# State-space sums in four row strips, head means as turned rows, and the tables of turns made earlier

## The chip, the cores and the metric

One core of a Trainium2 chip runs the whole program. The metric is the device time of one execution in microseconds (us); the figure for a kernel is the median of its runs. The engines are TensorE (PE), whose loads of the stationary operand are a row of their own (PEld), VectorE (DVE), ScalarE (ACT), GpSimd (POOL) and SyncE (SP), which issues most transfers.

## The reference, cut to what matters

Two hybrid layers (attention, convolution, retention, MLP), and then a second block: differential attention on queries and keys that are normed for each head and rotated, beside a state-space branch, then a gated MLP. The change lies in the projection part of the second block:

```python
q = rope(rmsnorm(q, q_norm_gain[i]), cos, sin)
k = rope(rmsnorm(k, k_norm_gain[i]), cos, sin)
...
bu_re = jnp.einsum('blgc,gpc->blgp', uf, bb_re)
bu_im = jnp.einsum('blgc,gpc->blgp', uf, bb_im)
_, _, xr, xi = lax.associative_scan(_complex_affine_combine, (ar, ai, bu_re, bu_im), axis=1)
y = (jnp.einsum('gcp,blgp->blgc', c_re, xr) - jnp.einsum('gcp,blgp->blgc', c_im, xi) + d_skip * uf)
```

The complex recurrence is done on every fourth position. Its input is turned back by an angle that grows with time (`sin_n`, `cos_n`), so that what is left to scan is real, and the result is turned forward again.

## The kernel before, in words

Weights come as f32 in units of 128x2048. ACT makes a rounded high part of each unit (`hi`, `w_hi`), POOL the rest (`lo`, L518, `w_lo`), and PE makes each product from three terms (L711, 128x512 each). All orders are written out by hand. In the q and k part, PE works through 32 accumulations of 12 matmuls each (four groups of `feature_major(4)`), and after accumulation p it calls `hook(p)`, which puts the small matmuls of the side work in between. ACT and DVE walk through the same p in programs of their own. A semaphore for each PSUM bank says that it is full (`full4`) or free (`free4`); each engine waits in program order.

The side work by p, on PE: `sums_in(blk)` at 8, 12, 16, 20 (L1010, input of the recurrence for a block of four strips of 32 rows); `sums_out(blk)` at 14, 18, 22, 26 (L1024 and L1031, output, bank 6); `short_response` at 10 (L995, bank 6); `q_columns(n)` at 9 and 17 (L1041, bank 7, means of q's squares as columns); `k_mean(j)` from 22 on (L1051, bank 7). On DVE: `states(blk, stage)` with stages 0, 1, 2 at the three p after each `sums_in` (L2341 to L2349 read the banks, L2355 is the scan, L2360 to L2366 make the state that `sums_out` needs); `skip(q)` (L2371, frees bank 6) one p after `sums_out`; `rotate(j)` (L2398, L2400, L2401) at 8, 8, 12, 12, 16, 16, 20, 20 for q, then for k with `k_norm`. At one p the order on DVE is skip, states, rotate, q_columns. On ACT at one p: `block_out`, `short_response` (four copies, L1723), then `jobs(p)`, which begins with `fetch_partner(j)`: four transfers (L1692) that need the rotation of block j-2 (`q_ready`), two such sets at p = 10 and at p = 18.

`sums_in` uses banks 4 and 5, a bank for each of the parts (real, imaginary). Two strips run at a time, and after each round PE waits (`strip_done`) so that two strips never write one bank together. POOL makes the tables `sin_n` and `cos_n` with `turns(b)`, six TENSOR_TENSOR each (L643 to L648), between the `lo` calls of this part, two buffers of each table, so that turns(2) and turns(3) wait for the states of blocks 0 and 1.

Of the kernel before, what the change touches and what calls it, by code (L numbers as in the profile page):

```python
# [186 lines left out]
def build(nc, a, out):  # L187

    with ExitStack() as ctx:
        m = memory(nc)  # L190
        m.bank = [ctx.enter_context(nc.psum_tensor(f"bank{i}", [P, T], F32)) for i in range(8)]
# [38 lines left out]
    "taps_clear", "u_ready", "strip_done", "spread", "kernel_made", "glu_done",  # L230
# [46 lines left out]
def memory(nc):  # L277
# [43 lines left out]
    def ar(name, shape, kb, dt=F32):  # L321
# [37 lines left out]
    m.b_part = ar("b_part", [P, T], 24)  # L359
# [6 lines left out]
    m.both = put("both", [P, T], at=x_at + 2048 * 5)  # L366
    m.sin_n, m.cos_n = ([put(f"{name}{i}", [P, T], at=x_at + 2048 * (6 + k) if i == 0 else arena + 1024 * (36 + 2 * k)) for i in range(2)]
                        for k, name in enumerate(("sin_n", "cos_n")))
# [3 lines left out]
    m.q_mean, m.q_power = (ar(name, [P, 2, 8, NT], 72 + 2 * i) for i, name in enumerate(("q_mean", "q_power")))  # L372
    m.g_hi, m.g_lo = (ar(f"gated{i}", [P, 4, T], 76 + 8 * i, F32R) for i in range(2))
# [123 lines left out]
def low_parts(pool, m, s):  # L497
# [89 lines left out]

    def layer(l):
# [17 lines left out]
        if l < DEPTH - 1:  # L606
            passes(pool, c, U_MLP // 2 - 2, PER_PAIR, pair)
        else:
            for _ in range(4):
                lo()  # L610
            for _ in output_tables():
                lo()
            for _ in range(U_MLP - 4 - 4 - 15):
                lo()
# [14 lines left out]
    def turns(b):  # L629

        shape = [P, 4, TURN_A, TURN_B]
        wide = lambda x: x[:].rearrange("p (s a b) -> p s a b", s=4, a=TURN_A)
        sin, cos, both = wide(m.sin_n[b % 2]), wide(m.cos_n[b % 2]), wide(m.both)
        of = slice(4 * b, 4 * b + 4)
        (sa, sb), (ca, cb) = ((x[:, of, 0:TURN_A].rearrange("p s (a o) -> p s a o", o=1).to_broadcast(shape),
                               x[:, of, TURN_A:].rearrange("p s (o b) -> p s o b", o=1).to_broadcast(shape)) for x in (m.sin_t, m.cos_t))
        if b == 0:

            pool.wait_ge(s["x_parked"], 16)
        if b >= 2:  # L640

            pool.wait_ge(s["state_ready"], 2 * (b - 1))
        pool.tensor_tensor(sin, sa, cb, ALU.mult)  # L643
        link(pool.tensor_tensor(both, ca, sb, ALU.mult))
        link(pool.tensor_tensor(sin, sin, both, ALU.add))
        pool.tensor_tensor(cos, ca, cb, ALU.mult)
        link(pool.tensor_tensor(both, sa, sb, ALU.mult))
        link(pool.tensor_tensor(cos, cos, both, ALU.subtract))  # L648
        pool.sem_inc(s["turned"], 1)


# [30 lines left out]
def products(pe, m, s):  # L682
# [316 lines left out]
    def sums_in(blk):  # L999

        fill(4)
        fill(5)
# [3 lines left out]
        for r in range(4):  # L1006
            for j in range(SUB):
                for part in range(2):
                    q = (r + part) % 4
                    mm = pe.matmul(bank[4 + part][:, q * P:(q + 1) * P], m.b_pow[strips[q], SUB - 1 - j, part, blk, :],  # L1010
                                   m.uT[strips[q], blk, j * N_SUB:(j + 1) * N_SUB], start=(j == 0), stop=(j == SUB - 1))
                    if j == SUB - 1:
                        mm.then_inc(s["strip_done" if r < 3 else f"full{4 + part}"], 1)
            if r < 3:
                pe.wait_ge(s["strip_done"], c.up("strip_done", 2))
# [19 lines left out]
    def q_columns(n):  # L1035
# [18 lines left out]
    def hook(p):  # L1054
# [4 lines left out]
        for blk in range(4):  # L1059
            if p == SUMS_IN_AT[blk]:  # L1060
                sums_in(blk)
            if p == SUMS_OUT_AT[blk]:
                sums_out(blk)
        for n in jobs_at(p, COLUMNS_AT):
# [205 lines left out]
COLUMNS_AT, COLUMN_ROOT_AT = (9, 17), 18  # L1270
# [39 lines left out]
def functions(act, a, m, s):  # L1310
# [362 lines left out]
    def block_out(b, j):  # L1673
# [4 lines left out]
        elif j >= 4:  # L1678
            act.wait_ge(s["q_columns"], j // 4)
        act.activation(m.q_square[j % 4][:], bank[b][:], ACT.Square).then_inc(s["q_squared"], 1)  # L1680
# [21 lines left out]
    def jobs(p):  # L1702

        for j in jobs_at(p, PARTNER_AT):
            fetch_partner(j)
        for n in jobs_at(p, COLUMNS_AT):
# [22 lines left out]
    for p in range(32):  # L1729
# [11 lines left out]
        if p in SUMS_IN_AT:  # L1741
            use(4, 5)
# [157 lines left out]
def arithmetic(dve, m, s):  # L1900
# [432 lines left out]
    def states(blk, stage):  # L2333

        w0, w1, w2 = (x[:] for x in m.w)
        sin, cos = m.sin_n[blk % 2][:], m.cos_n[blk % 2][:]
        if stage == 0:
            dve.wait_ge(s["turned"], blk + 1)
            full(4)
            full(5)  # L2340
# [3 lines left out]
            link(dve.tensor_tensor(w1, bank[5][:], sin, ALU.mult))  # L2344
            link(dve.tensor_tensor(w0, w0, w1, ALU.add))
            dve.tensor_tensor(w1, bank[5][:], cos, ALU.mult).then_inc(s["free5"], 1)
            freed(4)
            freed(5)
# [62 lines left out]
    def jobs(p):  # L2411

        for j in jobs_at(p, ROTATE_AT):
            rotate(j)
        for n in jobs_at(p, COLUMNS_AT):
# [272 lines left out]
```

## Time and profile before

| what | value |
| --- | --- |
| median of 3 runs | 2146.66 us (2142.12 to 2146.75) |
| the profiled execution, its own time | 2144.72 us |
| its span in the trace | 2142.9 us |
| PE busy | 98% of the span |
| DVE, ACT, POOL busy | 50%, 41%, 43% |
| mean granted TensorE clock | 0.99 |

Busy shares are over the whole span. What the change touches lies at 1270 to 1430 us of the trace, and there the shares are others. A row of a timeline has the start in us, the duration in us, the engine, the line, the operation with its operands, and the count; in brackets stands how long the engine was idle before it, and what it waited for.

### The profile page before, as it was taken

The page shows a single profiled execution, that of the slowest core. Times are in us where ns is not written, and L with a number is a line of the kernel's source. Part 1 is how long each engine was busy: PE and PEld are TensorE (multiplying, and loading weights), DVE is VectorE, ACT ScalarE, POOL GpSimd, SP SyncE. Part 2 cuts the span into 40 slices and gives each one's busy share as a digit, 9 for nine tenths or more (in the row PEclk, how much of TensorE's full clock was granted, in tenths as well). Part 3 has the DMA queues.
Part 4 walks back from the last instruction along what each step waited for, and adds up shares of the span by engine and source line. Part 5 has one row for each costly group of instructions (what it writes and reads, how often), then busy time and mean ns, then how long its engine had stood idle before and what let it go on. Part 6 is the DMA issues. An engine that isn't in the chain of part 4 may idle for free.

```text
span 2142.9 us, 27507 instructions
## 1 busy us (share of the span) xinstructions
PE 2100.7 (98%) x10200; PEld 1676.2 (78%) x10200; DVE 1061.5 (50%) x1725; ACT 876.3 (41%) x1219; POOL 925.4 (43%) x306
## 2 busy tenths in 40 slices
PE   8999999999999999999999999999999899999999
PEld 7875888888888776888888888877766787888887
DVE  5866242222247654422222258985588534554555
ACT  5345462223243445533222343164566534333332
POOL 5522444443455333545654456333312254444442
PEclk9999999999999999999999998899999999999999
DMA  5431213223224331233222242223111232322232
GB/s 182 150 117 71 77 63 98 97 98 98 99 69 149 125 93 46 79 99 98 94 100 87 92 148 85 66 84 108 60 60 60 95 100 81 97 88 90 97 98 78
DMA packets 120050, 202.29 MB, mean 94 GB/s; under 512 B 6544, under 2 KB 51856, under 8 KB 119696
## 3 DMA queue, kind: packets, MB, share of 16 engines
q1 hardware_dynamic: 112992, 189.12, 26.7%
q10 hardware_dynamic: 6960, 11.88, 1.9%
q8 instruction: 60, 0.98, 0.2%
q14 instruction: 38, 0.31, 0.0%
HBM read 189.44 MB, written 8.12 MB: 92 GB/s over the span
## 4 chain that ended last, share of the span: by engine, by line
PE 75%; issue 16%; POOL 3%; DVE 3%; ACT 1%; ACTq 1%; DMA 0%; POOLq 0%; DVEq 0%; SPq 0%
PE bank L711 63%; PE bank L813 5%; POOL w_lo L518 3%; PE bank L822 1%; PE bank L1010 1%; PE bank L765 1%; PE bank L840 1%; PE bank L880 1%; PE bank L774 1%; PE bank L868 0%; ACTq L1572 0%; DVE pr L2018 0%; PE bank L1041 0%; ACTq L1692 0%; PE bank L906 0%
## 5 line engine op out<-in xcount | busy, mean ns | idle before, releaser
L518 POOL TENSOR_TENSOR w_lo<-raw,w_hi 128x2048 fp32r<-128x2048 f32 (+1 forms) x167 | 741.9, 4442 | 1119.3 <-ACT w_hi L1356 1119.3
L711 PE MATMUL bank<-act_hi,w_hi 128*128 128x512 f32 x1488 | 595.6, 400 | 5.9 <-DVE hid L2561 2.5
L711 PE MATMUL bank<-act_hi,w_lo 128*128 128x512 f32 x1488 | 584.7, 393 | 0.0
L711 PE MATMUL bank<-act_lo,w_hi 128*128 128x512 f32 x1488 | 584.1, 393 | 0.0
L1356 ACT ACTIVATE w_hi<-raw 128x2048 fp32r<-128x2048 f32 (+1 forms) x170 | 314.2, 1848 | 591.2 <-PE bank L711 545.8
L711 PEld LDWEIGHTS bank<-act_hi,w_hi 128*128 128x128 f32 x1488 | 282.5, 190 | 78.0 <-issue 11.8
L711 PEld LDWEIGHTS bank<-act_hi,w_lo 128*128 128x128 f32 x1488 | 281.9, 189 | 60.7
L711 PEld LDWEIGHTS bank<-act_lo,w_hi 128*128 128x128 f32 x1488 | 282.5, 190 | 58.2 <-issue 1.4
L711 PE MATMUL bank<-h_hi,w_hi 128*128 128x512 f32 x704 | 277.7, 394 | 0.3 <-DVE x L2526 0.3
L711 PE MATMUL bank<-h_lo,w_hi 128*128 128x512 f32 x704 | 277.4, 394 | 0.0
L711 PE MATMUL bank<-h_hi,w_lo 128*128 128x512 f32 x704 | 277.4, 394 | 0.0
L2263 DVE TENSOR_TENSOR f<-f,bank 128x512 f32<-128x512 f32 x128 | 88.1, 688 | 238.7 <-PE bank L711 238.7
L2249 DVE SCALAR_TENSOR_TENSOR hid<-bank,rrow 128x512 f32<-128x512 f32 x64 | 43.7, 691 | 250.3 <-PE bank L711 245.3
L711 PEld LDWEIGHTS bank<-h_hi,w_hi 128*128 128x128 f32 x704 | 131.7, 187 | 33.4 <-DVE h_lo L2080 0.7
L711 PEld LDWEIGHTS bank<-h_hi,w_lo 128*128 128x128 f32 x704 | 131.7, 187 | 32.7
L711 PEld LDWEIGHTS bank<-h_lo,w_hi 128*128 128x128 f32 x704 | 131.7, 187 | 32.1
L2556 DVE TENSOR_TENSOR bank<-bank,rrow 128x512 f32<-128x512 f32 x44 | 30.7, 699 | 142.9 <-PE bank L711 140.4
L813 PE MATMUL bank<-act_hi,w_hi 128*128 128x512 f32 x192 | 76.3, 398 | 5.7 <-DVE act_lo L1940 5.2
L534 POOL TENSOR_TENSOR sums<-sums,squares 128x512 f32<-128x512 f32 x50 | 64.6, 1292 | 37.4 <-ACT squares L1374 35.1
L1993 DVE SCALAR_TENSOR_TENSOR bank<-ypad,lcol,bank 128x512 f32<-128x512 f32 x116 | 76.6, 755 | 0.0
L813 PE MATMUL bank<-act_hi,w_lo 128*128 128x512 f32 x192 | 74.8, 390 | 0.0
L813 PE MATMUL bank<-act_lo,w_hi 128*128 128x512 f32 x192 | 74.8, 389 | 0.0
(362 smaller groups left out, 2638.5 us busy)
## 6 DMA issues: line engine op xcount, KB each, us to landing
raw<-in_w_up SPq DMA_DIRECT2D x32, 1024.0 KB, 5.4
raw<-in_w_down SPq DMA_DIRECT2D x32, 1024.0 KB, 5.0
raw<-in_w_in SPq DMA_DIRECT2D x26, 1024.0 KB, 5.1
raw<-in_w_up SPq DMA_DIRECT2D x44, 512.0 KB, 4.6
raw<-in_w_in SPq DMA_DIRECT2D x28, 768.0 KB, 4.5
raw<-in_w_out SPq DMA_DIRECT2D x12, 1024.0 KB, 5.0
raw<-in_w_down SPq DMA_DIRECT2D x22, 512.0 KB, 4.2
raw<-in_w_attn_proj SPq DMA_DIRECT2D x4, 1024.0 KB, 5.1
```

What stands on the lines that cost most here:

```text
L518: pool.tensor_tensor(m.w_lo[slot][:, 0:n], m.raw[slot][:, 0:n], m.w_hi[slot][:, 0:n].bitcast(F32), ALU.subtract).then_inc(s["split_ready"], 1)
L534: ins = pool.tensor_tensor(m.sums[:], m.sums[:], m.squares[n % 4][:], ALU.add)
L711: mm = pe.matmul(o, ll if i == 2 else lh, rl if i == 1 else rh, start=first and n == 0, stop=last and n == len(steps) - 1)
L765: mm = pe.matmul(bank[b][:, t:t + 1], x[:, t * P:(t + 1) * P], m.per_d, start=(part == 0), stop=(part == 1))
L774: mm = pe.matmul(bank[b][:, t * P:(t + 1) * P], column[:, t:t + 1].to_broadcast([P, P]), m.ident, start=True, stop=True)
L813: mm = pe.matmul(bank[b][:], (wl if i == 2 else wh)[:, k % KU, cols], (m.act_lo if i == 1 else m.act_hi)[:, k, :], start=(k == 0 and i == ...
L822: pe.matmul(bank[b][:] if o is None else o, lhsT, rhs, start=True, stop=True).then_inc(s[f"full{b}"], 1)
L1356: act.activation(m.w_hi[slot][:, 0:n], m.raw[slot][:, 0:n], ACT.Copy).then_inc(s["w_hi"], 1)
L1993: ins = dve.scalar_tensor_tensor(to, y, w, sums, ALU.mult, ALU.add)
L2249: dve.scalar_tensor_tensor(m.hid[:, b, :], bank[b][:], 0.0, m.rrow[:], ALU.max, ALU.mult).then_inc(s[f"free{b}"], 1)
L2263: dve.tensor_tensor(sums, sums, bank[4 + b][:], ALU.add).then_inc(s[f"free{4 + b}"], 1)
L2556: dve.tensor_tensor(bank[b][:], bank[b][:], m.rrow[:], ALU.mult).then_inc(s["up_scaled"], 1)
```

## The change

`sums_in` now gives each of the four row strips a bank of its own (banks 4 to 7, one tensor of four banks), real part in columns 0 to 127, imaginary part in 128 to 255. The rounds and their waits go. All four banks must be free before it, and DVE frees all four after its last read of stage 0.

q's means: `q_rows` (p = 10 and 18) makes one matmul of 512 columns for each of the four squares, into a column strip of bank 7; ACT copies the bank into `q_rows`; `q_columns` (p = 11 and 19) turns it with four matmuls. There were 32 matmuls for each n before. The root of the columns moves from p = 18 to p = 20.

The tables have four buffers. turns(0) is made in the MLP of the second layer, in three pieces between `lo` calls; turns(1) stands behind the second layer's norm ahead of the `lo` that turns(0) followed before; turns(2) and turns(3) stand where turns(0) and turns(1) stood. Only turns(3) waits for `x_parked`. ACT's `block_out(7)` waits for all four.

```diff
+        m.quad = ctx.enter_context(nc.psum_tensor("bank4", [P, 4, T], F32))
+        m.bank += [m.quad[:, i, :] for i in range(4)]
...
-    m.b_part = ar("b_part", [P, T], 24)
+    m.b_part = ar("b_part", [P, T], 10)
...
+            lo()
+            for _ in turns(0):
+                lo()
+            for _ in range(U_MLP - 4 - 4 - 15 - 3):
                 lo()
...
     lo()
     pool.wait_ge(s["arena_free"], DEPTH + 1)
     pool.memset(m.taps[:], 0.0).then_inc(s["taps_clear"], 1)
-    pool.wait_ge(s["trig_ready"], 2)
+    whole(turns(1))
     lo()
-    turns(0)
+    whole(turns(2))
     lo()
-    turns(1)
-    lo()
-    turns(2)
-    lo()
-    turns(3)
-    lo()
-    lo()
+    whole(turns(3))
+    for _ in range(4):
+        lo()
     lo()
...
     def sums_in(blk):
-        fill(4)
-        fill(5)
+        for b in QUAD:
+            fill(b)
...
-        for r in range(4):
+        for part in range(2):
             for j in range(SUB):
-                for part in range(2):
-                    q = (r + part) % 4
-                    mm = pe.matmul(bank[4 + part][:, q * P:(q + 1) * P], m.b_pow[strips[q], SUB - 1 - j, part, blk, :],
+                for q, b in enumerate(QUAD):
+                    mm = pe.matmul(bank[b][:, part * P:(part + 1) * P], m.b_pow[strips[q], SUB - 1 - j, part, blk, :],
                                    m.uT[strips[q], blk, j * N_SUB:(j + 1) * N_SUB], start=(j == 0), stop=(j == SUB - 1))
...
+    def q_rows(n):
         pe.wait_ge(s["q_squared"], c.up("q_squared", 4))
         fill(7)
         for j in range(4):
-            for t in range(NT):
-                mm = pe.matmul(bank[7][:, 0:8 * NT].rearrange("p (c j t) -> p c j t", c=2, t=NT)[:, :, j, t], m.q_square[j][:, t * P:(t + 1) * P],
-                               m.blk64.rearrange("p (c d) -> p c d", c=2)[:, :, 0], start=True, stop=True)
+            mm = pe.matmul(bank[7][strips[j], :], m.blk64.rearrange("p (c d) -> p c d", d=4)[:, :, 0], m.q_square[j][:], start=True, stop=True)
+        mm.then_inc(s["full7"], 1)
+
+    def q_columns(n):
+        fill(7)
+        for t in range(NT):
+            mm = pe.matmul(bank[7][:, 0:8 * NT].rearrange("p (c j t) -> p c j t", c=2, t=NT)[:, :, :, t], m.q_rows[:, t * P:(t + 1) * P],
+                           m.ident.rearrange("p (j c d) -> p j c d", j=4, c=2)[:, :, :, 0], start=True, stop=True)
         mm.then_inc(s["full7"], 1)
...
-COLUMNS_AT, COLUMN_ROOT_AT = (9, 17), 18
+QUAD = (4, 5, 6, 7)
+ROWS_AT, COLUMNS_AT, COLUMN_ROOT_AT = (10, 18), (11, 19), 20
...
         for j in jobs_at(p, PARTNER_AT):
             fetch_partner(j)
+        for n in jobs_at(p, ROWS_AT):
+            evac(7, m.q_rows[:])
...
-            dve.tensor_tensor(w0, bank[4][:], cos, ALU.mult).then_inc(s["dve_step"], 1)
-            dve.tensor_tensor(w2, bank[4][:], sin, ALU.mult).then_inc(s["free4"], 1)
+            dve.tensor_tensor(by_strip(w0), re, by_strip(cos), ALU.mult).then_inc(s["dve_step"], 1)
+            dve.tensor_tensor(by_strip(w2), re, by_strip(sin), ALU.mult)
...
+            link(dve.tensor_tensor(by_strip(w1), im, by_strip(cos), ALU.mult))
+            for b in QUAD:
+                dve.sem_inc(s[f"free{b}"], 1)
```

## Rows read from the trace of the kernel before

**Rows 1.** The page: busy time of each engine, share of the span

```profile
PE 2100.7 (98%) x10200; PEld 1676.2 (78%) x10200; DVE 1061.5 (50%) x1725; ACT 876.3 (41%) x1219; POOL 925.4 (43%) x306
```

**Rows 2.** Windows: length, busy time of each engine, granted clock, DMA share

```profile
1290.00:1380.00 90.00, 88.89 (x732) 74.16 (x731) 79.43 (x92) 19.04 (x25) 54.59 (x29) 0.86 0.26 81
```

**Rows 3.** Timeline of PE, the small matmuls of p = 8 to 14

```profile
1296.73 5.93 PE L1010 MATMUL bank<-uT,b_pow 32*128 32x128 f32 x64
...
1307.48 4.15 PE L1041 MATMUL bank<-cmat,q_square 128*128 128x2 f32 x32
...
1316.89 2.09 PE L995 MATMUL bank<-ctab,braw 128*32 128x128 f32 x64
...
1324.58 4.92 PE L1010 MATMUL bank<-uT,b_pow 32*128 32x128 f32 x64
...
1335.00 2.39 PE L1024 MATMUL bank<-uT,taps 128*128 128x128 f32 x20
1337.32 1.52 PE L1031 MATMUL bank<-state,ctab 128*32 128x128 f32 x48
```

**Rows 4.** Timeline of PE, one of the large matmuls at each clock

```profile
1304.47 0.63 PE L711 MATMUL bank<-act_lo,w_hi 128*128 128x512 f32 x1
...
1320.63 0.39 PE L711 MATMUL bank<-act_lo,w_hi 128*128 128x512 f32 x1
```

**Rows 5.** Timeline of DVE, 1268 to 1405 us

```profile
1268.74 2.47 DVE L2288 TENSOR_TENSOR uT<-bank,rrow 128x512 f32<-128x512 f32 x2
...
1299.65 0.86 DVE L2398 TENSOR_TENSOR partner<-partner,rope 128x512 f32<-128x512 f32 x1 [3.59 <-DMA partner<-q]
...
1313.34 0.69 DVE L2346 TENSOR_TENSOR w<-bank,cos_n 128x512 f32<-128x512 f32 x1
...
1325.61 0.69 DVE L2398 TENSOR_TENSOR partner<-partner,rope 128x512 f32<-128x512 f32 x1 [3.65 <-DMA partner<-q]
...
1329.51 4.99 DVE L2401 TENSOR_TENSOR q<-q,partner 128x512 f32<-128x512 f32 x1
...
1338.86 5.25 DVE L2355 TENSOR_TENSOR_SCAN w<-par,w 128x128 f32<-128x128 f32 x8
...
1353.24 0.69 DVE L2398 TENSOR_TENSOR partner<-partner,rope 128x512 f32<-128x512 f32 x1
...
1361.50 0.69 DVE L2341 TENSOR_TENSOR w<-bank,cos_n 128x512 f32<-128x512 f32 x1
...
1366.00 2.63 DVE L2355 TENSOR_TENSOR_SCAN w<-par,w 128x128 f32<-128x128 f32 x8
...
1377.84 0.69 DVE L2398 TENSOR_TENSOR partner<-partner,rope 128x512 f32<-128x512 f32 x1
...
1379.90 0.69 DVE L2398 TENSOR_TENSOR partner<-partner,rope 128x512 f32<-128x512 f32 x1
...
1404.26 0.69 DVE L2366 TENSOR_TENSOR state<-state,w 128x508 f32<-128x508 f32 x1
```

**Rows 6.** Timeline of POOL, one low part and the first step of turns(3)

```profile
1328.78 5.17 POOL L518 TENSOR_TENSOR w_lo<-raw,w_hi 128x2048 fp32r<-128x2048 f32 x1 [14.33 <-ACT w_hi L1356]
...
1353.28 1.56 POOL L643 TENSOR_TENSOR sin_n<-turn_table,turn_table 128x512 f32<-128x512 f32 x1 [0.62 <-DVE state L2366]
```

**Rows 7.** Timeline of ACT at p = 10

```profile
1319.13 2.44 ACT L1723 ACTIVATE taps<-bank 32x512 f32<-32x512 f32 x4 [18.27 <-PE bank L995]
1321.68 5.01 ACTq L1692 DMA_DIRECT2D partner<-q  x8
```

**Rows 8.** Timeline of PE: a wait at p = 30, and a wait with what follows

```profile
1423.38 1.10 PE L1051 MATMUL bank<-q_square,cmat 128*128 128x512 f32 x2 [1.32 <-DVE q_square L2073]
...
1678.02 0.50 PE L711 MATMUL bank<-act_hi,w_hi 128*128 128x512 f32 x1 [2.30 <-DVE act_lo L2080]
...
1679.05 0.62 PE L711 MATMUL bank<-act_lo,w_hi 128*128 128x512 f32 x1
```

**Rows 9.** Windows: a stretch of the second layer's MLP

```profile
960.00:1000.00 40.00, 40.00 (x176) 32.49 (x175) 10.59 (x16) 12.00 (x12) 24.45 (x10) 1.00 0.25 79
```

More of the change, by code:

```diff
@@ L190, in build @@
         m = memory(nc)
-        m.bank = [ctx.enter_context(nc.psum_tensor(f"bank{i}", [P, T], F32)) for i in range(8)]
+        m.bank = [ctx.enter_context(nc.psum_tensor(f"bank{i}", [P, T], F32)) for i in range(4)]
+        m.quad = ctx.enter_context(nc.psum_tensor("bank4", [P, 4, T], F32))
+        m.bank += [m.quad[:, i, :] for i in range(4)]
         m.x_park = nc.dram_tensor("x_park", (P, NT * D), F32, kind="Internal").ap()
@@ L365, in memory @@
     m.state = [put(f"state{i}", [P, 4, N_SUB], at=x_at + 2048 * (3 + i)) for i in range(2)]
-    m.both = put("both", [P, T], at=x_at + 2048 * 5)
-    m.sin_n, m.cos_n = ([put(f"{name}{i}", [P, T], at=x_at + 2048 * (6 + k) if i == 0 else arena + 1024 * (36 + 2 * k)) for i in range(2)]
-                        for k, name in enumerate(("sin_n", "cos_n")))
+    m.both = ar("both", [P, T], 14)
+    m.sin_n, m.cos_n = ([ar(f"{name}{i}", [P, T], at + 2 * k) for i, at in enumerate((36, 28, 24))] +
+                        [put(f"{name}3", [P, T], at=x_at + 2048 * (5 + k))] for k, name in enumerate(("sin_n", "cos_n")))
     m.q_square = [ar(f"q_square{i}", [P, T], 56 + 2 * i) for i in range(4)]
@@ L372, in memory @@
     m.q_mean, m.q_power = (ar(name, [P, 2, 8, NT], 72 + 2 * i) for i, name in enumerate(("q_mean", "q_power")))
+    m.q_rows = ar("q_rows", [P, T], 92)
     m.g_hi, m.g_lo = (ar(f"gated{i}", [P, 4, T], 76 + 8 * i, F32R) for i in range(2))
@@ L586, in output_tables, with turns, whole @@
         pool.sem_inc(s["ctab_made"], 1)
+    def turns(b):
+        shape = [P, 4, TURN_A, TURN_B]
+        wide = lambda x: x[:].rearrange("p (s a b) -> p s a b", s=4, a=TURN_A)
+        sin, cos, both = wide(m.sin_n[b]), wide(m.cos_n[b]), wide(m.both)
+        of = slice(4 * b, 4 * b + 4)
+        (sa, sb), (ca, cb) = ((x[:, of, 0:TURN_A].rearrange("p s (a o) -> p s a o", o=1).to_broadcast(shape),
+                               x[:, of, TURN_A:].rearrange("p s (o b) -> p s o b", o=1).to_broadcast(shape)) for x in (m.sin_t, m.cos_t))
+        if b == 0:
+            pool.wait_ge(s["trig_ready"], 2)
+        if b == 3:
+            pool.wait_ge(s["x_parked"], 16)
+        pool.tensor_tensor(sin, sa, cb, ALU.mult)
+        link(pool.tensor_tensor(both, ca, sb, ALU.mult))
+        yield
+        link(pool.tensor_tensor(sin, sin, both, ALU.add))
+        pool.tensor_tensor(cos, ca, cb, ALU.mult)
+        yield
+        link(pool.tensor_tensor(both, sa, sb, ALU.mult))
+        link(pool.tensor_tensor(cos, cos, both, ALU.subtract))
+        pool.sem_inc(s["turned"], 1)
+    def whole(steps):
+        for _ in steps:
+            pass
     def layer(l):
@@ L627, in low_parts @@
         layer(l)
[L629 to L649, printed above, removed]
     lo()
@@ L1063, in hook @@
                 sums_out(blk)
+        for n in jobs_at(p, ROWS_AT):
+            q_rows(n)
         for n in jobs_at(p, COLUMNS_AT):
@@ L1705, in jobs @@
             fetch_partner(j)
+        for n in jobs_at(p, ROWS_AT):
+            evac(7, m.q_rows[:])
         for n in jobs_at(p, COLUMNS_AT):
@@ L1741, in functions @@
         if p in SUMS_IN_AT:
-            use(4, 5)
+            use(*QUAD)
         if p in SUMS_OUT_AT:
@@ L2414, in jobs @@
             rotate(j)
+        for n in jobs_at(p, ROWS_AT):
+            use(7)
         for n in jobs_at(p, COLUMNS_AT):
```

26 lines of the change are left out of this document (12 added, 14 removed).

## The prediction

> **What bounds the kernel now.** I read the page first: PE is busy 98% of the span [rows 1], so nearly everything that PE does is on the path, and small matmuls count in full. Then the windows over the part that is changed: in 1290 to 1380 us PE is still busy 88.89 of 90 us, but DVE is busy 79.43 of 90, and the granted clock is 0.86 [rows 2]. Two of the 1.2 and 2.4 GHz levels mixed to 0.86 mean 28% of the stretch, 25 us, at half clock. A large matmul there takes 0.63 us in place of 0.39 [rows 4]. The reader is to see that two engines are near full here, and that a saving on one of them is worth only what the other lets through. Last the timelines of PE, DVE, POOL and ACT, to see who is late at which p. At p = 30 PE waits 1.32 us for DVE [rows 8], and before it the third state (its last step at 1404.26 [rows 5]) is ready just in time for `sums_out(3)`. So by the end of the part DVE already sets the pace.
>
> **What PE saves by itself.** `sums_in` takes 4.92 us at full clock [rows 3], 0.077 us for each of 64 matmuls, waits between rounds included. No row shows four row strips at once. The nearest below is L1031, four column strips: 1.52 us for 48, 0.032 each, so 2.0 us. The bound above is L1024, whole-array matmuls of the same width: 2.39/20 = 0.12 us each, so 7.6 us. I take 2.0, since two strips already beat 0.12 by more than a third. Four blocks save 4 x 2.9 = 11.6 us. `q_columns` is 32 matmuls, 4.15 us [rows 3]; in its place stand four of 512 columns in column strips (by L1024 four times 4 x 0.12 = 1.9 us if they go one after another, 0.5 if side by side) and four turning ones, 0.5 us. I take 1.1 in all, so 2 x 3.0 = 6.0 us. If the half clock went too, PE would have 25/2 = 12.6 us more. Together that is 30 us. The Trainium skill (TensorE: Matmul & The Clock Gate, LDWEIGHTS) speaks against the first term: it says that a load of 32x128 weights takes as long as one of 128x128, since the columns count. By it `sums_in` would take 64 x 128/1.2 GHz = 6.8 us as an estimate, longer than now; the trace has 0.077 us a matmul with two strips, less than such a load of 0.107, so it doesn't bear that out for strips that overlap.
>
> **Why it doesn't arrive.** The banks. `sums_in` now takes banks 6 and 7 as well, and DVE frees all four only at the end of its stage-0 reads. So `short_response` (bank 6) and `q_rows` (bank 7) at p = 10 wait for states(0, 0), which they didn't; `sums_out(0)`, `(1)`, `(2)` wait for stage 0 of blocks 1, 2, 3; `sums_in(1)` waits for DVE's q_columns(0), `sums_in(2)` and `(3)` for skip(0) and skip(1). Behind each waiting matmul stand all large ones.
>
> Start of the part. turns(1) now lies at about 1278 to 1285 us, beside DVE's 18 steps for `b_pow`. Steps of POOL and of DVE that read only SBUF hold each other up: six DVE steps beside turns(3) (begun at 1353.28 [rows 6]) lasted 1353.24 to 1361.50, 8.26 us, where two rotates alone take 2 x 2.06 = 4.12 (1377.84 to 1379.90 is one) [rows 5]. That is 0.7 us a step; three to four steps of `b_pow` are hit, so it ends 2 to 3 us later, and `sums_in(0)` starts at 1299 instead of 1296.73 [rows 3]. It ends at 1301; two accumulations of (1335.00 - 1329.50)/2 = 2.8 us (1329.50 is the end of the second L1010 [rows 3]) bring PE to p = 10 at 1306.6. DVE is no earlier than before, because it waited for a transfer until 1299.65 [rows 5] and then has the same two rotates beside the same `lo` and a turns: its last bank read ends at 1313.34 + 0.69 = 1314.0 [rows 5]. PE waits 7.4 us.
>
> After a wait of 2.30 us large matmuls went at 0.62 [rows 8], half clock. So I take half clock for L995: 4.2 us for 2.09 [rows 3], end 1318.3. On ACT the copy of q_rows stands behind the taps (2.44 us) and behind eight transfers (5.01 us) [rows 7]: 1318.3 + 2.5 + 5.0 + 0.6 (one of the four copies of rows 7) = 1326.4. PE's q_columns is in order at 1327.3, DVE's at 1327.6, and only then come rotates 2 and 3, which began at 1325.61 [rows 5]. That is 2.1 us later. Were the clock full, it would be 1325.3, 0.3 earlier. `sums_in(1)` waits for the same step.
>
> From there DVE is the chain, and I keep its ledger up to 1404.26 [rows 5]. Off: the scans of block 1 ran beside turns(2), 5.25 us against 2.63 [rows 5], so -2.6, with 0.2 on the step before them; the six steps beside turns(3), -4.1. Sum -6.9. The long hits of `lo` stay (4.99 us for a step of 0.69 at 1329.51, beside 1328.78 + 5.17 [rows 5, 6]): `lo` is moved with PE, not removed. On: the later start, +2.1. New waits: `sums_out` can start only when stage 0 is over and takes 4.2 us (1335.00 to 1337.32 + 1.52 [rows 3], and 16 more matmuls at 0.03), while DVE has 0.7 + 2.7 us of block work before skip needs it, so about 1 us each at skip(0) and skip(1), +2.0. At skip(2) DVE has k's rotate and norm in between, no wait. Stage 0 reads four banks in runs of 128 columns: I take 0.69 as now (nothing added); the bound above is L2288, whose reads of PSUM with a stride take 2.47/2 = 1.24 [rows 5], 0.55 more x 16 reads = 8.8 us. Four `sem_inc` a block are under 0.3 us, in the range. Sum: -6.9 + 2.1 + 2.0 = -2.8 us at p = 26, and the same at p = 30, where PE waits for DVE in either kernel.
>
> turns(0) costs nothing in the MLP: with the output tables, the same kind of steps, between the `lo` there, PE is busy 40.00 of 40 us and POOL 24.45 [rows 9]; if the cover were gone, a late `lo` would cost its 2.6 us once or twice. `block_out(7)` waits for turns(3), which ends near 1314, 25 us ahead. No transfer is added. Behind p = 30 both orders are the same, PE is ahead of nothing new, and I carry the 2.8 us to the end.
>
> The sum against the profiled execution is 2144.72 - 2.8 = 2141.9 us. That execution is 1.9 under the median of its kernel, so for the median I say 2146.66 - 2.8 = 2143.9.
>
> **The rivals.**
> - *A, the forecast:* DVE's order sets the time, 2143.9; its own range is 2140 to 2148 (full clock at p = 10 gives 2.4, waits at skip that are twice as long cost 2). Chance 0.50.
> - *B, DVE gives more.* The clock stays full at p = 10 (2.4), the 1 us waits vanish (2.0), and a `lo` falls on bank reads instead of SBUF steps once (4.3 us, 4.99 - 0.69): 2.8 + 8.7 = 11.5, so 2135; half of it gives 2140. For it speaks that two `lo` more or less in phase decide it; against, that the one shown hit in full [rows 5, 6], as did four more like it in the stretch. Chance 0.20.
> - *C, slower: half clock at the output sums.* PE waits some 2 to 5 us before `sums_out(0)`, `(1)` and `(2)`, and a wait of 2.30 was enough [rows 8]. Each at half clock is 4.2 us more, and skip hangs on it. One costs 4.2 (2148.1), two 8.4 (2152.3), three 12.6 (2156.5). It decides from three on. For it: the idle times; against: 5.5 us of large matmuls before each wait. The Trainium skill (TensorE: Matmul & The Clock Gate, Part 1) has the same mechanism, idleness between bursts brings the half rate back. Chance 0.14, of this 0.08 over the 0.3%.
> - *D, the strips don't overlap, or strided bank reads are dear.* 7.6 us a block puts PE behind DVE again: 4 x (7.6 - 4.9) = 10.8, less 6.0 for the means and part of the clock: near 2149; dear reads give 2143.9 + 8.8 = 2152.7. Chance 0.08. The Trainium skill's rule on weight loads (TensorE: Matmul & The Clock Gate, LDWEIGHTS) would be this case.
> - *E, no change:* what is won at p = 30 is lost at a later wait for DVE or ACT. 2146.7. Chance 0.08.
>
> **How the numbers follow.** 0.3% is 6.4 us, about what this measurement can tell from nothing. Faster (under 2140.2): B, most of it, and the edge of A: 0.21. Slower (over 2153.1): 0.08 of C, 0.03 of D: 0.11. Same: 0.68. The range goes from the far end of B, 2135, to two output sums at half clock, 2152.
>
> **What the profile after would show.** Right: the busy time of L1010 near 2 us a block and L1041's successor near 1 us, yet PE idle some 7 us before L995 with DVE L2346 as releaser, then 3 to 5 us before q_columns (ACT), and 1 to 5 us before the L1024 groups; DVE without a gap from 1328 on, no scan over 3 us; `k_mean(4)` at about 1420.5 instead of 1423.38. Wrong: PE without waits in the part (then B or more), or L711 at 0.63 us after each L1024 group (C), or L1010 groups over 5 us (D).

## The result, and the profile after

The changed kernel takes 2154.08 us (median of 8 runs, 2147.85 to 2155.78), the kernel before 2145.12 us (median of 8, 2142.12 to 2148.65) in the same set of runs. The ratio is 1.0035, with a 95% interval of 1.0025 to 1.0046: slower by 0.25 to 0.46%. Forecast were 2143.9 us and a range of 2135 to 2152. The profiled execution took 2151.82 us, its span is 2150.0.

The page's busy times of the changed kernel, against [rows 1]:

```profile
PE 2089.4 (97%) x10168; PEld 1666.4 (78%) x10168; DVE 1055.3 (49%) x1725; ACT 876.5 (41%) x1221; POOL 922.1 (43%) x306
```

TensorE has 11.3 us less to do and the kernel is 7.1 us longer in these two profiles. The windows view of the changed kernel, the stretch of [rows 2] with the same columns:

```profile
1290.00:1380.00 90.00, 70.13 (x636) 57.00 (x635) 69.00 (x92) 19.75 (x25) 35.35 (x17) 0.87 0.25 71
```

TensorE is busy 70.13 of 90 us where it was busy 88.89, at the same granted clock (0.87 against 0.86). So the saved work was replaced by waits and the half clock stayed. TensorE's waits between 1290 and 1430 us (engine and line, releaser: us in total, times, longest):

```profile
PE bank L1000 <- DVEq L2365: 10.2, 1, 10.2
PE bank L1026 <- DVEq L2365: 8.1, 2, 5.7
PE bank L1049 <- ACT q_rows L1372: 4.0, 1, 4.0
PE bank L1059 <- DVE q_square L2088: 1.4, 1, 1.4
```

Before, the same view had one line, the wait of 1.3 us at p = 30 [rows 8]. The timeline of TensorE in the changed kernel, against [rows 3] (L1014 is `sums_in`, L1000 the short response, L1042 `q_rows`, L1049 `q_columns`, L1026 and L1033 `sums_out`):

```profile
1298.59 2.07 PE L1014 MATMUL bank<-uT,b_pow 32*128 32x128 f32 x64
1316.53 3.64 PE L1000 MATMUL bank<-ctab,braw 128*32 128x128 f32 x64 [10.20 <-DVEq L2365]
1319.94 1.65 PE L1042 MATMUL bank<-q_square,cmat 128*32 128x512 f32 x8
1328.54 1.66 PE L1049 MATMUL bank<-cmat,q_rows 128*128 128x8 f32 x7 [3.99 <-ACT q_rows L1372]
...
1366.18 4.64 PE L1026 MATMUL bank<-uT,taps 128*128 128x128 f32 x20 [5.68 <-DVEq L2365]
1370.75 2.29 PE L1033 MATMUL bank<-state,ctab 128*32 128x128 f32 x48
...
1390.95 2.50 PE L1026 MATMUL bank<-uT,taps 128*128 128x128 f32 x20 [2.39 <-DVEq L2365]
```

The strips overlap: 64 matmuls take 2.07 us, 0.032 each, where two strips took 4.92. What follows them is waits for L2365, the `sem_inc` with which VectorE hands back the four banks, and half clock behind the longer ones (4.64 us for what takes 2.39 at full clock). VectorE in the changed kernel, against [rows 5]:

```profile
1301.77 0.92 DVE L2415 TENSOR_TENSOR partner<-partner,rope 128x512 f32<-128x512 f32 x1 [3.55 <-DMA partner<-q]
...
1315.53 0.69 DVE L2363 TENSOR_TENSOR w<-bank,cos_n 128x512 f32<-128x512 f32 x1
1316.65 0.69 DVE L2366 TENSOR_TENSOR w<-w,w 128x512 f32<-128x512 f32 x1 [0.43 <-DVE w L2363]
...
1330.54 0.19 DVE L2398 SCALAR_TENSOR_TENSOR q_mean<-small,bank 128x32 f32<-128x32 f32 x1 [6.57 <-PE bank L1049]
1330.87 4.59 DVE L2415 TENSOR_TENSOR partner<-partner,rope 128x512 f32<-128x512 f32 x1
...
1343.37 2.63 DVE L2372 TENSOR_TENSOR_SCAN w<-par,w 128x128 f32<-128x128 f32 x8
1347.33 0.75 DVE L2388 SCALAR_TENSOR_TENSOR uT<-uT,scol,bank 128x512 f32<-128x512 f32 x1 [1.33 <-PE bank L1033]
...
1356.09 0.69 DVE L2415 TENSOR_TENSOR partner<-partner,rope 128x512 f32<-128x512 f32 x1 [1.89 <-DMA partner<-q]
1356.70 5.08 DVE L2417 TENSOR_TENSOR q<-q,rope 128x512 f32<-128x512 f32 x1
...
1373.63 0.75 DVE L2388 SCALAR_TENSOR_TENSOR uT<-uT,scol,bank 128x512 f32<-128x512 f32 x1 [3.96 <-PE bank L1033]
```

The scans of block 1 are down to 2.63 us from 5.25, as forecast. VectorE itself now waits: 6.57 us for the means, 1.33 and 3.96 us for output sums.

### The profile page after: what moved, and what is told of

It is laid out like the page before. It is cut to its first block, busy times and chain, and to the rows that moved or that the text cites. A ratio compares the mean times of both kernels' runs of the same rounds, so it can differ in the third digit from the quotient of the medians.

```text
span 2150.0 us, 27464 instructions
## 1 busy us (share of the span) xinstructions
PE 2089.4 (97%) x10168; PEld 1666.4 (78%) x10168; DVE 1055.3 (49%) x1725; ACT 876.5 (41%) x1221; POOL 922.1 (43%) x306
## 4 chain that ended last, share of the span: by engine, by line
PE 73%; issue 16%; DVE 5%; POOL 3%; ACT 1%; ACTq 1%; DMA 1%; DVEq 0%; POOLq 0%
PE bank L716 61%; PE bank L818 5%; POOL w_lo L521 3%; PE bank L827 1%; PE bank L770 1%; PE bank L845 1%; PE bank L794 1%; DVE q L2417 1%; PE bank L885 1%; PE bank L779 1%; ACTq L1705 1%; PE bank L873 0%; ACTq L1583 0%; PE bank L1026 0%; DVE pr L2033 0%
```

## One part of the span, in all profiles

Executions of one kernel differ by some us even outside the change, so I compare a part: from the first matmul of `spread` (1271.06 in the changed kernel) to the first attention product (1517.30), 246.24 us. Before, it runs from 1269.20 to 1511.60, 242.40 us. Here it is for every profile taken, beside the granted clock of 1290 to 1380 us from the windows view (the stretch of [rows 2]):

| kernel | granted clock : part in us, one pair a profile |
|---|---|
| before | 0.86 : 242.4; 0.98 : 235.6; 0.98 : 235.9 |
| changed | 0.87 : 246.2; 0.89 : 246.5 |
| changed, copy first | 0.91 : 244.8 |
| changed, copy first, other order | 0.89 : 244.2 |
| changed, idle products: many, fitted | 0.98 : 255.7; 0.94 : 246.1 |
| changed, copy first, rotations after the read | 0.94 : 236.6 |
| tables only | 0.98 : 231.6; 0.94 : 235.0; 0.90 : 239.7; 0.87 : 242.7 |
| four strips only | 0.82 : 268.7 |
| tables and rows, two banks, copy second | 0.94 : 235.2; 0.91 : 239.2 |
| tables and rows, two banks, copy first | 0.98 : 230.4; 0.94 : 234.8 |
| the same, rotations after the read | 0.91 : 236.5 |

The first line matters most. The profile that the prediction was read from has the longest part of three: its part is 6.5 to 6.8 us longer than in the other two. The whole time hides this, since what differs outside the part made up for it (the first profile spent 631.3 us behind the part and 1269.2 ahead of it, the second 634.3 and 1276.3).

## The experiments

Times are medians, each beside runs of the kernel before on the same chip; ratios carry 95% intervals.

**Taking the change apart.** The tables alone (sums in the two old banks, the old 32 products for the means):

```
-ROWS_AT, COLUMNS_AT, COLUMN_ROOT_AT = (10, 18), (11, 19), 20
+COLUMNS_AT, COLUMN_ROOT_AT = (9, 17), 18
-        for b in QUAD:
-            fill(b)
+        fill(4)
+        fill(5)
...
```

> Only the tables of turns are made earlier (four buffers); sums_in keeps two banks and its rounds, q's means keep their 32 matmuls. Theory 1 (the four banks tie PE to DVE, the tables only relieve DVE): no wait of PE before L995 or the output sums, no scan over 3 us beside a turns, DVE about 5 to 7 us earlier at its last state step (1404.26 before), k_mean(4) at 1417 to 1420; time 3 to 6 us under the kernel before, ratio about 0.998. Rival (the loss comes from the tables' new place, beside DVE's b_pow steps): sums_in(0) 2 to 3 us late and the time 2 to 4 us over.

The four strips alone, put into the kernel before:

```
-        fill(4)
-        fill(5)
+        for b in QUAD:
+            fill(b)
...
```

> Only sums_in goes to four strips in four banks; the tables and q's means stay as before. Theory 1: q_columns(0) and short_response wait 7 us and more for stage 0, output sums wait again, nothing is gained on DVE: time 6 to 12 us over the kernel before, ratio 1.003 to 1.006. Rival (the strips' PE time arrives, the loss is elsewhere): time 3 to 8 us under.

Tables and rows together, `sums_in` in banks 4 and 5 as before:

> The changed kernel with sums_in back in two banks with rounds (tables early, q's means as turned rows). Theory 1: the wait before L995 is gone; PE still waits some us before q_columns(0), since the copy of q_rows stands behind eight transfers on ACT; DVE gains as with the tables alone: time 2 to 6 us under the kernel before. Rival (turned rows cost by the ACT wait as much as they save): as the kernel before, within 2 us.

Tables alone: 2150.77 against 2143.80, ratio 1.0027 (1.0010 to 1.0045). Strips alone: 2174.17, ratio 1.0132 (1.0108 to 1.0155). Tables and rows: 2148.34, ratio 1.0020 (1.0003 to 1.0037). So the strips are the part that costs most. The tables alone, and tables with rows, missed their expectations: they were expected 2 to 6 us under the kernel before and came out 7.0 and 4.5 over. These two are timed again below. TensorE's waits in the kernel with strips alone, 1290 to 1480 us, say what the strips cost (L1040 is its `q_columns`, L1023 its `sums_out`, L2350 the release of the four banks):

```profile
PE bank L1040 <- DVEq L2350: 20.9, 2, 12.2
PE bank L1023 <- DVEq L2350: 12.9, 2, 8.4
```

The means use bank 7 and the output sums bank 6. Both stand behind VectorE's read of all four banks, and on VectorE that read stands behind two rotations. Four times 2.9 us saved on TensorE buy 33.8 us of waits. With the tables and the means changed as well, the part is 22 us shorter than with the strips alone (246.2 against 268.7).

**Idle products in the waits.** Is it the waits or the half clock behind them? Matmuls of 128 columns that nobody reads were put ahead of the three long waits of the changed kernel:

```
+        if p in FILLERS:
+            b, n = FILLERS[p]
+            emptied(b)
+            for _ in range(n):
+                pe.matmul(bank[b][:, 0:P], m.ident, m.ident, start=True, stop=True)
```

> The changed kernel with filler matmuls of the identity (their results are never read) while PE waits: 80 before short_response, 30 before q_columns(0), 40 before sums_out(1). Theory 2 (half clock after the waits makes the loss): granted clock 1.00 in 1300 to 1380 us, L1000 in 2.1 us instead of 3.6, the wait of DVE for skip(1) falls from 4.0 to about 1 us, k_mean(4) 4 to 6 us earlier than in the changed kernel, time about 1.001 of the kernel before. Theory 1 alone: the waits stay as long, time within 2 us of the changed kernel, about 1.003.

The first had 80, 30 and 40 of them: 2159.32, ratio 1.0067 (1.0043 to 1.0090). It was badly sized. Its timeline of TensorE shows the first group (two array passes for each product):

```profile
1306.27 18.02 PE L1069 MATMUL bank<-cmat 128*128 128x128 f32 x160
```

That is 18.0 us in a wait of 10.2, so only the 0.98 of its clock can be used. The second had 44, 17 and 24:

> The changed kernel with 44, 17 and 24 idle products of 128 columns (0.22 us each by the earlier run) on TensorE ahead of its three long waits, so that they end about when the waits do. No work is taken away, and TensorE is never idle there for more than 1 to 2 us. If the half clock behind the waits is what costs (the output sums of the second block at 4.6 and 2.7 us in place of 2.4 and 2.0), the stretches at half clock in the part fall from 23.8 us to under 8 and the kernel takes 3 us less (2151). If the waits themselves cost, it stays at 2154 within 1 us. The earlier run had too many of them (18 us in a wait of 10) and can't tell the two apart.

It took 2147.75 against 2143.49, ratio 1.0020 (1.0005 to 1.0034). Its TensorE at the second block:

```profile
1363.15 5.52 PE L1069 MATMUL bank<-cmat 128*128 128x128 f32 x48
1368.79 2.50 PE L1026 MATMUL bank<-uT,taps 128*128 128x128 f32 x20
1371.22 1.52 PE L1033 MATMUL bank<-state,ctab 128*32 128x128 f32 x48
```

These output sums run at full clock. They begin 2.6 us later than in the changed kernel and end 0.3 us earlier. The start is late for two reasons. `b_pow` was late in this execution, `sums_in(0)` waited 2.0 us for it. And the first group of idle products was still too long, as VectorE's last read of block 0 and the short response show:

```profile
1316.79 0.69 DVE L2369 TENSOR_TENSOR w<-bank,cos_n 128x512 f32<-128x512 f32 x1
1319.80 1.96 PE L1000 MATMUL bank<-ctab,braw 128*32 128x128 f32 x64
```

L1000 begins 2.3 us after the end of that read. In the changed kernel it begins 0.3 us after it, so the idle products cost some 2.0 us there themselves. The part is unchanged (246.1), the timed ratio is 0.0015 lower, and the two intervals overlap. So up to 3 us by the times may be the clock, and some 2 us more if the idle products had ended with the wait, out of 7.5 us. This run doesn't tell the waits from the clock; it shows that the part is no shorter with the clock of 1290 to 1380 us at 0.94.

**The copy first.** ScalarE copies q's rows ahead of issuing eight transfers:

```
-        for j in jobs_at(p, PARTNER_AT):
-            fetch_partner(j)
         for n in jobs_at(p, ROWS_AT):
             evac(7, m.q_rows[:])
+        for j in jobs_at(p, PARTNER_AT):
+            fetch_partner(j)
```

> The changed kernel with ACT copying q's rows ahead of the eight partner transfers that it issues at the same step. If the wait of 4.0 us at TensorE's second product of q's means (behind the copy, which stood behind 5.0 us of transfers being issued) is part of the loss, TensorE does that product 3.5 to 4.5 us earlier, VectorE's wait of 1.3 us ahead of the first skip goes, and the kernel takes 1 to 2.5 us less than the changed one (2152 to 2153). If VectorE's own order sets the part, the wait only moves to the next product and the time stays at 2154 within 1 us. If it is the clock, the half-clock stretch near 1328 us goes with the wait, and the gain is up to 4 us.

> The tables of turns and the turned rows as in the change, the sums in the two old banks, and the copy of the rows first. Against the same kernel with the copy second (2148.3) it should be 1 to 4 us shorter (2144 to 2147) if the 4.6 us wait there is on the path, and equal within 1 us if it is hidden. If the time is made by what lies outside the part (the stretches at half clock near 1239 and 1640 us), it stays at 2148 whatever the part does.

Both ran on one chip, with before at 2143.49. With four banks: 2150.71, ratio 1.0026 (1.0012 to 1.0041). With two: 2138.68, ratio 0.9974 (0.9958 to 0.9990). They differ in nothing but the banks and strips of `sums_in` with the reads and signals that belong to them, and by 12.0 us. TensorE with four banks:

```profile
1321.26 3.55 PE L1000 MATMUL bank<-ctab,braw 128*32 128x128 f32 x64 [8.34 <-DVEq L2365]
...
1344.02 3.72 PE L1026 MATMUL bank<-uT,taps 128*128 128x128 f32 x20 [4.09 <-DVEq L2365]
...
1368.79 4.18 PE L1026 MATMUL bank<-uT,taps 128*128 128x128 f32 x20 [5.46 <-DVEq L2365]
```

and with two (L1015 is `sums_in`, L1029 `sums_out`):

```profile
1302.55 4.92 PE L1015 MATMUL bank<-uT,b_pow 32*128 32x128 f32 x64
...
1313.06 1.96 PE L1000 MATMUL bank<-ctab,braw 128*32 128x128 f32 x64
...
1332.80 2.39 PE L1029 MATMUL bank<-uT,taps 128*128 128x128 f32 x20
```

The two-bank kernel pays 4.92 us for its sums and nothing behind them. In the four-bank kernel the wait for the copy is gone as expected, but a wait of 4.09 us stands at `sums_out(0)` instead, and the median is 3.4 us under the changed kernel's from another set of runs (ratio 1.0026 against 1.0035, overlapping). TensorE's waits in the part come to 24.7 us, against 24.8 in the changed kernel: they moved.

**Another order, with four banks.** Rows ahead of the first sums, the short response at p = 9, the first sums at p = 10. The copy is first here too, and at one p VectorE reads the means ahead of its rotations:

```
-ROWS_AT, COLUMNS_AT, COLUMN_ROOT_AT = (10, 18), (11, 19), 20
+ROWS_AT, COLUMNS_AT, COLUMN_ROOT_AT = (8, 18), (9, 19), 20
-ROTATE_AT = (8, 8, 12, 12, 16, 16, 20, 20)
+ROTATE_AT = (8, 9, 12, 12, 16, 16, 20, 20)
...
-SHORT_AT = 10
-SUMS_IN_AT, SUMS_OUT_AT = (8, 12, 16, 20), (14, 18, 22, 26)
+SHORT_AT = 9
+SUMS_IN_AT, SUMS_OUT_AT = (10, 12, 16, 20), (14, 18, 22, 26)
-STATES_AT = ((9, 10, 11), (13, 14, 15), (17, 18, 19), (21, 22, 23))
+STATES_AT = ((10, 11, 12), (13, 14, 15), (17, 18, 19), (21, 22, 23))
...
```

> The changed kernel with its steps in another order: q's rows ahead of the first state sums, the short response between them and the columns, the first state sums after both, and the second rotation after the first means. No product of TensorE then needs one of the four banks while the first block's sums are in them, so the wait of 10.2 us at the short response and the 4.0 us at the columns should go. If these waits (and the half clock behind them) are what the four banks cost, the part is 4 to 8 us shorter than in the changed kernel and the whole takes 2146 to 2150. If VectorE's order sets everything, it is 2152 to 2155 as before it.

It took 2147.36, ratio 1.0013 (1.0000 to 1.0026), in the range expected, but its part is only 2 us shorter than the changed kernel's, where 4 to 8 were expected, and 0.6 shorter than with the copy first alone. The 10.2 us wait went from L1000 and stands, as 11.65, at the next user of bank 6 (L1028 is `sums_out` here, L2367 the release):

```profile
1334.87 4.64 PE L1028 MATMUL bank<-uT,taps 128*128 128x128 f32 x20 [11.65 <-DVEq L2367]
```

**The read ahead of the rotations.** This is the test of the shared banks: the same four banks, strips, reads and signals, with each pair of rotations one step later, so that VectorE reads first.

```
-ROTATE_AT = (8, 8, 12, 12, 16, 16, 20, 20)
+ROTATE_AT = (9, 9, 13, 13, 17, 17, 21, 21)
```

> The changed kernel, copy first, with every pair of rotations one step later, so that VectorE reads a block's state sums out of the four banks ahead of the two rotations and not behind them. If the shared banks 6 and 7 are what costs, TensorE's waits of 10.2, 5.7 and 2.4 us fall to under 2 us each, the part takes 232 to 238 us (246 in the changed kernel) and the whole 2138 to 2144. If it is the form of the reads or the four signals, the waits go but the part stays above 242 us. If the rotations then come late for the partner transfers, ScalarE's issue of the next ones moves back and the second means are late by some 5 us, with a time near 2147.

> The same move of the rotations in the kernel with tables and rows and the two old banks (2138.7 without the move). There TensorE has no wait for the read, so the move should bring nothing: 2137 to 2141. If it costs through the partner transfers, it is 2142 or more; what it costs here is to be taken off the result with four banks.

Both on one chip, with before at 2144.76. Four banks: 2142.93, ratio 0.9989 (0.9975 to 1.0003). Two banks: 2140.89, ratio 0.9981 (0.9965 to 0.9996). With the old order the four banks cost 12.0 us against two; now they cost 2.0, and the two intervals overlap. Against the same kernel with the old order the ratio falls from 1.0026 to 0.9989 and the part from 244.8 to 236.6. TensorE with four banks:

```profile
1309.56 1.95 PE L1000 MATMUL bank<-ctab,braw 128*32 128x128 f32 x64 [0.61 <-DVEq L2365]
...
1329.95 3.80 PE L1014 MATMUL bank<-uT,b_pow 32*128 32x128 f32 x64 [11.01 <-DVE q_mean L2398]
...
1358.95 2.50 PE L1026 MATMUL bank<-uT,taps 128*128 128x128 f32 x20 [2.02 <-DVEq L2365]
```

The waits of 8.3, 4.1 and 5.5 us are 0.6, 0 and 2.0. One of 11.0 us is left, and it is the other shared bank: `sums_in(1)` needs bank 7, which holds q's means until VectorE, behind rotations, scans and stage 2, has read them. The expectation missed it. A four-bank kernel without that wait wasn't tried. The windows view over the whole part, for four and two banks with the old order and then four and two with the rotations later (length, busy time of TensorE, ..., granted clock):

```profile
1275.64:1520.43 244.79, 219.36 (x1505) 174.09 (x1504) 173.20 (x206) 96.72 (x120) 97.67 (x34) 0.96 0.33 103
1275.01:1505.41 230.40, 224.08 (x1505) 177.36 (x1504) 176.01 (x206) 96.77 (x120) 96.89 (x34) 0.99 0.35 110
1271.70:1508.29 236.59, 214.30 (x1506) 169.92 (x1505) 172.12 (x206) 96.95 (x120) 95.47 (x34) 0.98 0.34 107
1271.57:1508.03 236.46, 230.11 (x1506) 182.27 (x1505) 162.49 (x206) 96.77 (x120) 96.11 (x34) 0.96 0.33 107
```

TensorE is idle for 25.4, 6.3, 22.3 and 6.4 us. Of the 8.2 us by which the part with four banks gets shorter, only 3.1 are idle time; 5.1 are busy time, at a granted clock of 0.98 against 0.96. How much the shorter waits gave by themselves and how much the clock behind them gave is not shown. That the parts with four and with two banks are equally long (236.6 and 236.5) is chance: with two banks this profile met more half clock than the first with the old order (0.96 against 0.99).

**The same kernels again.** For the clock's part in it, profiles were taken a second time.

> The changed kernel once more, for a second profiled execution. If the stretches at half clock outside the part (near 874, 1239 and 1649 us, 13.6 us of them more than in the profile of the kernel before) are the change's, they stand there again; if they are chance, some are gone and the time is 1 to 3 us less. The 10.2 us wait at the short response and the 5.7 us wait at the second output sums should be there within 1 us either way: they are VectorE's order and not the clock's.

> The kernel with the tables alone once more. Its profiled execution took 2134.5 us and was its fastest of twelve (median 2150.8). If its usual execution loses to the clock, this one shows 15 to 25 us more at half clock than the first and the waits of the first; if it loses to a wait or a transfer that comes and goes, the granted clock is the same and one wait is 10 us longer.

> The same once more, for the same question: where the half clock stands in an execution of the usual length. By the clock's theory the part from spread to the first attention product takes 8 to 16 us more than the 231.6 us of the first, with the slow stretches in or right behind it; by chance outside the part, the part stays at 232 us and the rest is longer.

> The kernel before once more, to see how much its own profile varies: the part took 242.4 us with 27.2 us at half clock inside it. If its order sets the part, it is 241 to 244 us again; if the slow stretches do, it moves by 0.5 us for each us more or less at half clock.

> The kernel before a third time. The part took 242.4 us with 27.2 us at half clock and 235.6 us with 3.4 us. It should be near one of the two again, by how much half clock it meets, and TensorE should have no wait in the part ahead of 1385 us either way.

> The kernel with tables, rows first and two banks once more. Its part took 230.4 us with 3.4 us at half clock. If the rows take enough off TensorE that it is no longer the bound, a second profile is at 230 to 236 us whatever half clock it meets; if TensorE is still the bound, it rises by 0.3 to 0.5 us for each us at half clock, as the tables alone did.

They took 2153.73, 2143.40, 2146.73, 2148.01, 2143.68 and 2141.03 us in this order; their parts stand in the table. The changed kernel's part is the same twice, 246.2 and 246.5. One of its waits isn't: L1000 waited 6.73 us in the second, against an expectation within 1 us of 10.2, since `sums_in(0)` itself had waited 1.91 us for VectorE and then ran at half clock (3.65 us in place of 2.07). The half clock outside the part, which the first profile of the changed kernel had more of than that of before, comes and goes: in 1225 to 1260 us the granted clock is 0.90 and 0.95 in the changed kernel and 1.00, 0.90 and 0.90 in the kernel before. Two rows of the windows view, each of a kernel that showed about 0.87 in another profile: the kernel before, its third profile,

```profile
1290.00:1380.00 90.00, 88.87 (x780) 74.53 (x779) 80.76 (x95) 23.92 (x32) 57.86 (x29) 0.98 0.28 84
```

and the tables alone, its first:

```profile
1290.00:1380.00 90.00, 88.88 (x839) 74.62 (x837) 80.36 (x110) 21.93 (x30) 38.46 (x17) 0.98 0.30 87
```

TensorE is busy 88.9 of 90 us in both, as in [rows 2], yet the rows count 780 and 839 matmuls in that time and not 732 (their mix differs a little, since the stretch lies otherwise in the order). That an engine is busy all the time says nothing of how much gets done. The tables alone give 4 us at 0.98 (231.6 against 235.6 and 235.9) and nothing at 0.86 to 0.87 (242.7 against 242.4). In the tables' four profiles the part grows by 11.1 us as the clock goes from 0.98 to 0.87; 0.11 of 90 us is 9.9 us of TensorE's time. So in that kernel TensorE is the bound of the part, in the main. The kernel before goes only from 235.8 to 242.4, since at the higher clock TensorE waits for VectorE at k's means (2.28 us at the first, where the first profile had none): there the two engines are near level, and there the tables give their 4 us.

**Timed again.** The tables alone had been timed slower than before although no profile of them showed a part more than 0.3 us longer than the longest of before:

> The kernel with the tables alone, timed again. If its loss is its own (it meets more half clock than before because of where its steps fall), it is again 5 to 9 us slower than before and its mean granted clock is again 0.002 lower. If that set of runs made it, it is 1 to 4 us faster than before, as its part in the profiles (231.6, 235.0 and 242.7 us against 235.6, 235.9 and 242.4) would have it.

> Tables and rows in two banks with the copy behind the transfers, timed again (2148.3 before, 2138.7 with the copy first). The wait for the copy is 4.6 us in its profile, part of it hidden, so by the waits it should take 2140 to 2143; if it is at 2147 or more again, the copy's place costs more than its wait, through the clock.

The tables alone took 2148.35 against 2144.34, ratio 1.0018 (0.9999 to 1.0036); tables and rows with the copy second 2147.23, ratio 1.0001 (0.9981 to 1.0022). The mean granted clock of the runs was 0.9877 for the tables and 0.9903 for before, as in the first set (0.9875 and 0.9898). So the tables' kernel meets half clock more often than the kernel before, in two sets on two chips, and this can eat its gain: 0.0023 and 0.0026 of 2144 us are 5 to 6 us, an estimate. The loss is smaller than I expected for that case (5 to 9 us), and its interval touches 1. Why its steps meet it more often stays open. Tables and rows at 2147.23 stand where the expectation put a cost of the copy's place through the clock, but their mean granted clock is 0.9902 against 0.9903 for before, so this set doesn't show the clock as the reason. With the copy first the same kernel had a ratio of 0.9974, against 1.0020 and 1.0001 with the copy second; that is 6 to 10 us, more than the wait of 4.6 us, and it stays open too.

## Why the prediction was wrong

**The step that failed** is the first: "by the end of the part DVE already sets the pace", and from it "From there DVE is the chain, and I keep its ledger". In the kernel before, TensorE had no wait from 1290 to 1423 us, and [rows 2] had it busy 88.89 of 90 us. It was the bound there, at a granted clock of 0.86; relieving VectorE by the tables alone gave nothing at that clock (242.7 us against 242.4). The ledger set 6.9 us of VectorE's savings against 4.1 us of delays (2.1 and 2.0) and never added up TensorE's own time. The windows view over the part does, before and changed:

```profile
1269.20:1511.60 242.40, 238.34 (x1537) 190.73 (x1536) 182.58 (x206) 95.85 (x118) 106.12 (x40) 0.94 0.32 104
1271.06:1517.30 246.24, 220.82 (x1505) 174.56 (x1504) 176.85 (x206) 96.86 (x120) 96.37 (x34) 0.95 0.32 103
```

TensorE has 17.5 us less to do, and is idle for 25.4 us in place of 4.1. Four waits are 22.3 us of these (10.2, 4.0, 5.7 and 2.4). So the part is 3.8 us longer where -2.8 was written. Kept along VectorE with the delays as measured, the ledger gives nearly the same, as the terms below show; so it is the price of the shared banks that was too low.

**The basis was off as well.** "The sum against the profiled execution" took a part of 242.4 us for the kernel's own. In two of three profiles it is 235.6 and 235.9. The changed kernel's part is 246.2 and 246.5, so it lies 4.0 us over the profile that I read and 10.6 over the other two. The timed difference, 9.0 us between the medians, is nearer the latter.

**Term by term**, by the two first profiles, with the 1.9 us taken off by which the changed one was already later at `spread`:
- `sums_in` at 2.0 us a block: right, 2.07. `q_rows` and `q_columns` at 1.1 together: 1.65 and 1.66 at half clock for the first means, 1.03 and 0.95 at full for the second, so low by 0.9 to 2.2.
- `b_pow` late by 2 to 3 us behind turns(1): not in the first profile (27.53 us from `spread` to the first sums in both kernels), but there in the second, a wait of 1.91. Right in kind, and it comes and goes.
- The wait at p = 10 of 7.4: 10.2 and 6.7. Half clock at L995's successor, 4.2: 3.64. `q_columns` at 1327.3: 1328.54, so 1326.7 with the 1.9 taken off.
- Rotates 2 and 3 later by 2.1: 3.4 (1330.87 - 1325.61 - 1.86).
- Savings on VectorE of 6.9: they came, 2.6 on the scans and 4.1 on the steps beside turns(3). Of the latter 1.9 went to a wait for the fifth partner's transfer, which the ledger didn't have. A faster engine reached a transfer that had been hidden.
- Waits at skip(0) and skip(1), "about 1 us each": 1.33 and 3.96. The second is behind output sums at half clock, and cost about 3 us more than forecast. This is one case of rival C, which would have decided from three on; its chain had one, so C isn't what happened.
- Four `sem_inc` "under 0.3 us": a pause of 0.43 us a block where the first three blocks had 0.1 before, so about 0.3.
- Strided reads of the banks at 0.69: right. Rival D is refuted in both halves.
- Of the signs: "DVE without a gap from 1328 on" is wrong (1.33, 1.89 and 3.96 us), and so is `k_mean(4)` at 1420.5. It began at 1429.03, later than before (1423.38).

Along VectorE, changed against before, the distance grows by 3.4 us up to rotate 2, -0.9 to stage 0 of block 1 (a `lo` hit of 4.59 for 4.99, and a transfer's wait of 0.55 less), -1.2 to skip(0), -2.1 to stage 0 of block 2, 3.9 to skip(1) and 0.4 behind it. That is +3.5 where -2.8 was written, and the part was +3.8. The largest single errors are 3.0 at skip(1), 1.9 for the transfer and 1.3 at the rotates, together 6.2 of the 6.3 us. What the terms could not show is that the part of before usually takes 6.6 us less than in the profile they were set against.

**What settles the cause.** Four banks against two, with the copy first in both, cost 12.0 us. With VectorE's reads ahead of the rotations in both, they cost 2.0 us, which is not clear of the noise. So banks 6 and 7, shared between the sums and what follows them and held until VectorE's read behind two rotations, are shown as the cause of some 10 us there. In the change itself the copy is second. There the two-bank kernel had ratios of 1.0020 and 1.0001 against 1.0035, so the four banks account for 3 to 7 of the 9.0 us; the rest lies with the tables and the copy's place, and is open. The prediction named the mechanism of the banks and priced it too low. The Trainium skill (TensorE: Matmul & The Clock Gate, LDWEIGHTS), that a load of 32x128 weights takes as long as one of 128x128, would have made 6.8 us of a block's sums as an estimate with the loads one after another; the trace has 2.07, so for four strips that sum of loads doesn't hold.

## What to carry to other kernels

When matmuls are spread over more banks to run faster, list who else uses those banks and what its reader stands behind in its engine's order; here 2.9 us saved in a block bought waits of up to 10 us, and moving two rotations behind the read took the cost of the four banks from 12.0 to 2.0 us. Where an engine is busy for the whole of a stretch without a wait, keep its ledger too, whatever the other is doing: here work taken off the other one brought nothing at the lower clock; and if the granted clock of that stretch is below 1, take a second profile before a forecast is built on it. The best kernel of the study leaves the sums in two banks, takes the tables and the turned rows, and copies the rows ahead of the transfers: 2138.68 us, 0.10 to 0.42% faster than before. It was timed once, and as the best of ten it may owe some of that to luck.

## What the runs showed of the hardware

- The same part of the same kernel had a granted clock of 0.86 in one execution and 0.98 in two others, without a wait of TensorE in any of them up to 1390 us. In the first of them the half clock set in inside groups of small matmuls: `sums_in` took 5.93 us and `q_columns` 4.15 [rows 3], and the large matmuls right behind each took 0.63 us. At full clock the groups take 4.92 and, in the third profile, 3.63.
- After a wait of 5.68 us the next 20 matmuls took 4.64 us in place of 2.39; with idle products in the wait 2.50. After waits of 2.39 and 2.02 us they took 2.50 as well, but after one of 2.31 us in the kernel with the other order 4.12.
- Four row strips in four banks gave 0.032 us for a matmul of 32x128 weights and 128 columns, against 0.077 for two strips with waits between the rounds.
- A low part on GpSimd held a single step of VectorE of 0.69 us for 4.6 to 5.1 us again and again, five times between 1300 and 1405 us in the first profile of each kernel, and once a group of scans (7.00 us for 2.63 in the kernel with the other order). The change moved these hits and removed none.
